# Split-precision matmuls in two passes per weight unit, high parts first and the low part last, with another order of loads and sums at the input stages' start

## The reference

```python
x = x + 0.5 * swiglu_ffn(x, ffn1_norm, ffn1_w_in, ffn1_w_out)   # D_FF = 5632
proj = rms_norm(x, mix_norm) @ w_in                             # q, k, v of 16 heads
# 8 heads: mixture of dilated windows; 8 heads: differential attention; RMS norm per head
x = x + mixed @ w_out
x = x + 0.5 * swiglu_ffn(x, ffn2_norm, ffn2_w_in, ffn2_w_out)

def swiglu_ffn(x, g, w_in, w_out):
    h = rms_norm(x, g)
    gate, up = jnp.split(h @ w_in, 2, axis=-1)
    return (jax.nn.silu(gate) * up) @ w_out
```

## Time and profile before

| | us |
|---|---|
| median of 3 runs | 1826.44 (1824.80 to 1827.83) |
| the profiled execution | 1826.57 |
| its span, first to last instruction | 1824.9 |
| PE busy in it | 1807.9 (99%) |
| DVE busy | 1519.9 (83%) |
| ACT busy | 1120.8 (61%) |

### The profile page before, as it was taken

One profiled execution on the slowest core, in us unless ns is written; L12 is line 12 of the kernel. 1 busy time (PEld: TensorE's weight loads), 2 busy tenths in 40 slices (PEclk: granted clock), 3 DMA queues, 4 the chain that ended last, 5 costly groups with the idle time before them and its releaser, 6 DMA issues.

```text
span 1824.9 us, 21558 instructions
## 1 busy us (share of the span) xinstructions
PE 1807.9 (99%) x8167; PEld 1475.5 (81%) x8167; DVE 1519.9 (83%) x1676; ACT 1120.8 (61%) x1437; POOL 78.9 (4%) x113
## 2 busy tenths in 40 slices
PE   9899999999999999999999999999999999999999
PEld 8688888888888888888888888788888888888887
DVE  6899999998889888667666666899999999889976
ACT  6666766666655555556556655566666666666453
POOL 0000000000000000111010000000000000000000
PEclk9999999999999999999999999999999999999999
DMA  9677776776545556654555445677777776554653
GB/s 361 183 245 221 238 246 218 228 226 202 182 171 206 209 207 209 207 180 149 171 165 183 152 161 193 229 237 246 243 224 241 241 228 189 186 184 162 237 201 139
DMA packets 184199, 378.62 MB, mean 207 GB/s; under 512 B 7824, under 2 KB 8864, under 8 KB 183840
## 3 DMA queue, kind: packets, MB, share of 16 engines
q1 hardware_dynamic: 178304, 351.02, 55.4%
q0 software_dynamic: 5760, 26.22, 7.5%
q10 hardware_dynamic: 32, 0.01, 0.0%
HBM read 348.91 MB, written 2.10 MB: 192 GB/s over the span
## 4 chain that ended last, share of the span: by engine, by line
PE 94%; DVE 3%; DMA 1%; issue 1%; SPq 1%; ACT 0%; POOL 0%; DVEq 0%; ACTq 0%; POOLq 0%
PE acc L587 13%; PE acc L588 13%; PE acc L589 13%; PE acc L649 6%; PE acc L650 6%; PE acc L651 6%; PE turn L665 5%; PE turn L667 5%; PE turn L668 5%; PE acc L665 4%; PE acc L667 4%; PE acc L668 4%; PE turn L618 1%; PE turn L787 1%; PE turn L786 1%; PE turn L788 1%
## 5 line engine op out<-in xcount | busy, mean ns | idle before, releaser
L1041 ACT ACTIVATE w_hi<-b 128x1024 fp32r<-128x1024 f32 (+1 forms) x300 | 268.8, 914 | 146.6 <-PE acc L651 113.4
L1436 DVE TENSOR_TENSOR w_lo<-b,w_hi 128x1024 fp32r<-128x1024 f32 (+1 forms) x300 | 298.1, 1043 | 53.5 <-ACT w_hi L1041 51.2
L1426 DVE TENSOR_TENSOR w_lo<-w_raw,w_hi 128x1024 fp32r<-128x1024 f32 x159 | 195.2, 1238 | 124.0 <-ACT w_hi L1017 123.5
L1017 ACT ACTIVATE w_hi<-w_raw 128x1024 fp32r<-128x1024 f32 x158 | 166.9, 1060 | 189.3 <-PE acc L589 166.7
L1055 ACT ACTIVATE w_hi<-w_raw 128x1024 fp32r<-128x1024 f32 x184 | 193.7, 1059 | 139.4 <-PE acc L589 96.4
L1446 DVE TENSOR_TENSOR w_lo<-w_raw,w_hi 128x1024 fp32r<-128x1024 f32 x184 | 223.1, 1222 | 43.0 <-ACT w_hi L1055 40.2
L587 PE MATMUL acc<-w_hi,h_hi 128*128 128x512 f32 x496 | 196.5, 396 | 0.2 <-DVE w_lo L1426 0.2
L589 PE MATMUL acc<-w_hi,h_lo 128*128 128x512 f32 x496 | 193.3, 390 | 0.0
L588 PE MATMUL acc<-w_lo,h_hi 128*128 128x512 f32 x496 | 193.2, 390 | 0.0
L649 PE MATMUL acc<-w_hi,h_hi 128*128 128x512 f32 x480 | 188.6, 393 | 0.3 <-DVE w_lo L1436 0.3
L588 PE MATMUL acc<-w_lo,act_hi 128*128 128x512 f32 x480 | 188.9, 393 | 0.0
(11 more groups left out here) (235 smaller groups left out, 3521.0 us busy)
## 6 DMA issues: line engine op xcount, KB each, us to landing
b<-in_ffn_w_in SPq DMA_DIRECT2D x80, 1280.0 KB, 5.8
w_raw<-in_ffn_w_out SPq DMA_DIRECT2D x88, 1024.0 KB, 5.5
w_raw<-in_ffn_w_in SPq DMA_DIRECT2D x54, 1024.0 KB, 5.3
w_raw<-in_w_in SPq DMA_DIRECT2D x48, 1024.0 KB, 5.1
w_raw<-in_ffn_w_in SPq DMA_DIRECT2D x44, 512.0 KB, 6.1
w_raw<-in_w_out SPq DMA_DIRECT2D x16, 1024.0 KB, 5.1
b<-t POOLq DMA_DIRECT2D x20, 768.0 KB, 7.8
b<-t POOLq DMA_DIRECT2D x20, 512.0 KB, 4.6
```

Of the source, the lines that this page charges most:

```text
L1017: nc.scalar.activation(w_hi[:, u % RING, 0:count, :], w_raw[:, slot, k0:k0 + count, :], ACT.Copy).then_inc(hi_ready, 1)
L1041: nc.scalar.activation(w_hi[:, u % RING, 0:count, :], in_raw(piece)[:, k0:k0 + count, :], ACT.Copy).then_inc(hi_ready, 1)
L1426: nc.vector.tensor_tensor(w_lo[:, slot, 0:count, :], w_raw[:, v // 2 % RAW, k0:k0 + count, :], w_hi[:, slot, 0:count, :].bitcast(F32), ALU ...
L1436: nc.vector.tensor_tensor(w_lo[:, u % RING, 0:count, :], in_raw(piece)[:, k0:k0 + count, :], w_hi[:, u % RING, 0:count, :].bitcast(F32), A ...
```

## The change

1. In `unit`, `plain_unit`, `form` and `out_form` a unit becomes two passes. PE waits for the high part only, issues hi x w_hi and lo x w_hi for all slices (and halves), then waits for the low part and issues hi x w_lo. The number of matmuls is the same. The first four units of IN1, written out apart, are not touched.
2. IN1's loads: chunk 6 moves ahead of B12 and chunk 7 ahead of B22 and B21.
3. IN2's loads: the four blocks move ahead of chunks 6 and 7.
4. On DVE the low parts of P1 come before `first_sum` (which `load_loop` then has to wait for by itself before B11 of the next loop), and `lambda_sums` comes after loop 0.
5. In a loop `make_u3` comes one low part earlier, before the last unit of P3.

```diff
                 if later:
+                    if i == 0:
+                        sp.wait_ge(sum_ready, (SUMS if s_in == IN2 else 0) + 1)
                     load_in(src, s_in, i + 1, B11, LAST[i, "P1"])
...
                 if s_in == IN2:
-                    load_first(gate_up, s_in)
-                    for piece in (B11, B12, B22, B21, G0, G1, U1, U0):
+                    load_first(gate_up, s_in, 0, RAW + 2)
+                    for piece in (B11, B12, B22, B21):
+                        load_in(gate_up, s_in, 0, piece)
+                    load_first(gate_up, s_in, RAW + 2)
+                    for piece in (G0, G1, U1, U0):
                         load_in(gate_up, s_in, 0, piece)
...
             load_first(gate_up1, IN1, RAW, RAW + 2)
-            for piece in (B11, B12):
+            load_in(gate_up1, IN1, 0, B11)
+            load_first(gate_up1, IN1, RAW + 2, RAW + 3)
+            load_in(gate_up1, IN1, 0, B12)
+            load_first(gate_up1, IN1, RAW + 3)
+            for piece in (B22, B21, G0):
                 load_in(gate_up1, IN1, 0, piece)
-            load_first(gate_up1, IN1, RAW + 2, RAW + 3)
-            for piece in (B22, B21):
-                load_in(gate_up1, IN1, 0, piece)
-            load_first(gate_up1, IN1, RAW + 3)
-            load_in(gate_up1, IN1, 0, G0)
...
             def unit(u, k0, count, lhs, bank, first, last, halves=False):
 
-                pe.wait_ge(lo_ready, u + 1)
                 slot = u % RING
+                pe.wait_ge(hi_ready, u + 1)
                 for kk in range(count):
                     for t in range(TT):
-                        hi, lo = (a[:, k0 + kk, t * P:(t + 1) * P] for a in lhs)
-                        o = banks[bank][:, t, :]
-                        nc.tensor.matmul(o, hi, w_hi[:, slot, kk, :], start=first[t] and kk == 0, stop=False)
-                        nc.tensor.matmul(o, hi, w_lo[:, slot, kk, :], start=False, stop=False)
-                        mm = nc.tensor.matmul(o, lo, w_hi[:, slot, kk, :], start=False,
-                                              stop=last[t] and kk == count - 1)
-                        if halves and kk == count - 1 and t == 0:
-                            mm.then_inc(first_half, 1)
+                        for n, a in enumerate(lhs):
+                            nc.tensor.matmul(banks[bank][:, t, :], a[:, k0 + kk, t * P:(t + 1) * P], w_hi[:, slot, kk, :],
+                                             start=first[t] and kk == 0 and n == 0, stop=False)
+                pe.wait_ge(lo_ready, u + 1)
+                for t in range(TT):
+                    for kk in range(count):
+                        mm = nc.tensor.matmul(banks[bank][:, t, :], lhs[0][:, k0 + kk, t * P:(t + 1) * P],
+                                              w_lo[:, slot, kk, :], start=False, stop=last[t] and kk == count - 1)
+                    if halves and t == 0:
+                        mm.then_inc(first_half, 1)
                 mm.then_inc(units_used, 1)
...
-                split_in_lo(s_in, LAST[i, "P6"] + 4, LAST[i, "P7"] + 4)
+                split_in_lo(s_in, LAST[i, "P6"] + 4, LAST[i, "P7"] + 3)
                 make_u3(s_in, n, i)
-                split_in_lo(s_in, LAST[i, "P7"] + 4, LAST[i, "GC"] + 1)
+                split_in_lo(s_in, LAST[i, "P7"] + 3, LAST[i, "GC"] + 1)
...
                     split_sums(n)
-                    lambda_sums()
                 else:
...
+                split_in_lo(s_in, 0, 3)
                 first_sum(s_in, n, 0)
-                split_in_lo(s_in, 0, 3)
...
                 for i in range(IN_LOOPS):
                     hidden(s_in, i, n)
+                    if n == 0 and i == 0:
+                        lambda_sums()
```

More of the change, by code:

```diff
@@ L658, in form @@
                     u = UNIT[s_in] + IN_FIRST + v
-                    pe.wait_ge(lo_ready, u + 1)
                     slot = u % RING
                     k0, count = IN_ORDER[v][3:]
+                    pe.wait_ge(hi_ready, u + 1)
                     for kk in range(count):
-                        hi, lo = lhs(k0 + kk)
-                        last = stop and k0 + kk == KS - 1
-                        nc.tensor.matmul(o, hi, w_hi[:, slot, kk, :], start=start and k0 + kk == 0, stop=False,
-                                         skip_group_check=True)
-                        nc.tensor.matmul(o, hi, w_lo[:, slot, kk, :], start=False, stop=False, skip_group_check=True)
-                        mm = nc.tensor.matmul(o, lo, w_hi[:, slot, kk, :], start=False, stop=last, skip_group_check=True)
+                        for n, a in enumerate(lhs(k0 + kk)):
+                            nc.tensor.matmul(o, a, w_hi[:, slot, kk, :], start=start and k0 + kk == 0 and n == 0,
+                                             stop=False, skip_group_check=True)
+                    pe.wait_ge(lo_ready, u + 1)
+                    for kk in range(count):
+                        mm = nc.tensor.matmul(o, lhs(k0 + kk)[0], w_lo[:, slot, kk, :], start=False,
+                                              stop=stop and k0 + kk == KS - 1, skip_group_check=True)
                     mm.then_inc(units_used, 1)
@@ L780, in out_form @@
             def out_form(u, lhs, o, start, stop):
+                slot = u % RING
+                pe.wait_ge(hi_ready, u + 1)
+                for kk in range(UK):
+                    for n, a in enumerate(lhs):
+                        nc.tensor.matmul(o, a[:, kk, :], w_hi[:, slot, kk, :], start=start and kk == 0 and n == 0, stop=False)
                 pe.wait_ge(lo_ready, u + 1)
-                slot = u % RING
                 for kk in range(UK):
-                    hi, lo = (a[:, kk, :] for a in lhs)
-                    nc.tensor.matmul(o, hi, w_hi[:, slot, kk, :], start=start and kk == 0, stop=False)
-                    nc.tensor.matmul(o, hi, w_lo[:, slot, kk, :], start=False, stop=False)
-                    mm = nc.tensor.matmul(o, lo, w_hi[:, slot, kk, :], start=False, stop=stop and kk == UK - 1)
+                    mm = nc.tensor.matmul(o, lhs[0][:, kk, :], w_lo[:, slot, kk, :], start=False, stop=stop and kk == UK - 1)
                 mm.then_inc(units_used, 1)
```

15 lines of the change are left out of this document (9 added, 6 removed).

## The result

| | before | after |
|---|---|---|
| median, us | 1825.62 (1824.73 to 1827.83, 4 runs) | 1810.64 (1810.57 to 1810.82, 4 runs) |
| span of the profiled execution | 1824.9 | 1809.1 |
| PE busy | 1807.9 | 1796.2 |

The ratio is 0.9916, with a 95% interval of 0.9899 to 0.9933: faster by 15.0 us. The forecast was 1809.1 in a range of 1800 to 1818. A negative number is a gain.

A forecast was written before the change was run, and what follows sets the result against it. TensorE, busy 99%, was taken as the bound, with only its holes to win. Terms -7.7 - 8.0 + 0.6 - 0.7 + 0.2 + 0.3 - 2 = -17.3 from 1826.57 gave 1809.3, by the median 1809.1 us; range 1800 to 1818.

The forecast's parts named there:

- Loops: Input-stage loops: PE's stalls for low parts at UA (18 x 0.23) and P7 (20 x 0.18) vanish, gaining 7.7 us.
- First start: Start of the first input stage: DVE's chain ends earlier, transposes after P2 at 67.9 instead of 75.95, gaining 8.0 us.
- Two parts are independent of each other: First input stage's start: moving `lambda_sums` and the earlier weight chunk each gain 3.8 us, independently.
- Added waits: About 920 new waits inside units, mostly on reached semaphores, cost 0.3 us for all.
- Rival (d): An added wait inside a unit costs as a stalled one does; all give 1809 + 74 = 1883 us; chance 0.03.
- Spacing: Steps between matmuls shrink because more followers stream from the same tile; -2 us taken, bounds -10 and +33.
- Rival (f): Matmul spacing doesn't depend on order within a unit but on where tiles lie; 1811.3 us, chance 0.20.
- (a): Only half the first input stage's start gain, as the chunk stays transfer-bound or DVE stalls elsewhere; 1813.3 us, chance 0.12.
- (b): Input loops don't get shorter: DVE at 92% sets them and the stall returns mid-unit; 1817.3 us, chance 0.12.
- (c): Slower: new pairs of load and stream cost more in the high pass; 1844 us, chance 0.05.
- (e): All matmuls take 389 ns, 10 us less; 1801 us, chance 0.05.
- (g): Gains and spacing cancel to within 0.2% (3.7 us); chance 0.03.

The follow-up runs named there:

- chunk_back: Changed kernel with the first input stage's loads in the order of before; 1813.45 us, ratio 0.9929.
- lambda_back: Changed kernel with `lambda_sums` put back behind `split_sums(n)`, ahead of the loops; 1817.34 us, ratio 0.9952.
- sum_early_2: Changed kernel with `first_sum` ahead of P1's low parts again in the second input stage only; 1809.22 us, ratio 0.9907.
- passes_only: Kernel before with only the units in two passes; loads, sums, `lambda_sums` and `make_u3` as before; 1816.31 us, ratio 0.9946.
- place_0: Changed kernel with gains and small vectors behind the large tiles, so act, mix, s_hi and raw weights begin at 0 modulo 1024; 1799.34 us, ratio 0.9852.
- best_order: Changed kernel with DVE's first sums earlier in both input stages and the first loop's third sum behind P2's low parts; 1811.81 us, ratio 0.992.
- best_all: best_order with tiles placed as in place_0 and the first loop's accumulating transfers waiting only for the sum they read; 1795.38 us, ratio 0.9836.

## Why the prediction was right, and where not

The total was 1809.1 for a measured 1810.64 (1.5 us off in 15.0, in the range). Against the profiled execution the sum was -17.3 and the trace shows -15.8. The close total owes something to luck: the loops gave 0.8 more than their term, the first start 0.8 less. Step by step:

- **Loops, -7.7.** Measured -8.5, of which 0.3 is the event at 228 us that the prediction did not count. The mechanism is shown by the runs: 41.37 with the passes alone, 41.80 with the order alone. The 0.23 and 0.18 per place (0.41 in a loop with both) came out as 0.43.
- **First start, -8.0.** Measured -7.2. The chain of 18.2 us measured 18.4 (49.97 to 68.40). It began 0.7 late. The sum had PE at unit 11 at 40.2, and it was there at 40.68, with no stall ahead of it. Of these 0.45 us, 0.11 is the restart, which the sum took off although it comes only after unit 11 has begun (the step into unit 11 was 0.63 in the trace of before, a stall of 0.40). The other 0.34 is there from the first microseconds on: one and the same matmul starts between 6.99 and 7.59 in the fourteen kernels here, and one and the same low part on DVE between 39.31 and 39.95; the term took one execution's start for exact. The last 0.2 is the time from the end of unit 11 on PE (43.40) to ScalarE's start on unit 15 (43.66), for which the sum had nothing.
- **"Two parts are independent of each other: 3.8 (lambda) and 3.8 (chunk)."** This step was wrong, though the sum was not. chunk_back and lambda_back show 2.6 for the chunk if `lambda_sums` is gone, and nothing if not. The row with the 3.07 us held the answer: a wait for a transfer ends at a time of its own, and what stands ahead of it can't be shortened with profit. The two had to be counted in that order: first the wait goes, then the chain behind it can move. Had the change left `lambda_sums` where it was, this step would have promised some 4.2 us at the first turn (8.0 - 3.8), where lambda_back has 0.7.
- **Second start, +0.6.** Measured +0.62; sum_early_2 shows the cause and takes it back.
- **The other wait, -0.7, and the end, +0.2.** Both as measured. A like wait at 654.77 in OUT1 (0.18 of the -0.26 there) was not in the sum.
- **Added waits, +0.3; make_u3, 0.** Measured 0.00: 138 of the 914 units with an added wait lie between 700 and 1130 us, and no turn moved against another there; at 0.08 each they would have cost 11 us. Rival (d) is out. `make_u3` was not undone by itself; the loops of passes_only (without it) and of the changed kernel are both 41.37, so it is worth nothing.
- **Spacing, -2.** Measured 0 in the output stages and between 700 and 1130 us; in the loops it can be no more than the 0.4 by which they gained more than the stalls. This is the mis-sized term: more than the whole 1.5 us of the miss. Rival (f), with 0.20, was right that the order within a unit doesn't matter, and its words on the cause, the differences "come from where the tiles lie", are borne out as far as place_0 goes. By the rule of the Trainium skill ("TensorE: Matmul & The Clock Gate", "Step-by-step: what each phase is for"), that loading the next weights takes no read bandwidth from the running matmul, this term was to be nothing, and the trace agrees (0.00 us from 700 to 1130 us with another order of loads and streams). The differences of 4 to 7 ns between the groups, which the prediction set against that rule, are averages over a pattern: on act the steps go 229.0, 231.2, 226.6 and again, in the old order and in the new. In the old one each kind of matmul fell on one place of that pattern, so the pattern showed up as a difference between lines (393, 392, 389); in the new one it spreads over them (392, 392, 391). The groups by line could not tell the two apart; the steps in order of time could. The high pass on act, at 392, is also where a sign of the prediction's list failed ("at or below 391"). And the term's two bounds don't belong together: +33 counts 7,440 matmuls from a middle of 391.5, from which all at 389 would be -19 and not -10.
- **Rivals (a) and (b)** did not come about, nor did (c), (e) and (g): the time is 9 us and more from the number of each of these three. In (a) it was the share of DMA that spoke for a chunk that stays late; the high parts of its units no longer waited for it. In (b) DVE's 92% is 93% now, and it costs nothing.

## What to carry to other kernels

A wait belongs where the data is first needed: a split of each unit into a pass on what is ready and a pass on what comes last hid some forty short stalls of 0.2 us, and its satisfied waits cost nothing that could be measured. Before two gains on one chain are added, ask which of them is a wait that ends at a time of its own; a gain ahead of it is worth nothing until it is gone. When steps differ by one or two per cent between tiles, look at where the tiles lie before explaining it by the order of instructions: here it was worth 11 us, three quarters of the whole change. And when work is moved back, look at who counts it: a queue that waits for "all sums" will follow, and can run into a load that has come forward.

## What the runs showed of the hardware that was not expected

- The step of matmuls with a weight load each depended on where tiles lie in a partition: 226.8 ns on act with act, mix, s_hi and the raw weights at 0 modulo 1024 bytes, 228.9 at 960, 232.7 to 233.4 at 896, 928 and 992. Moving these tiles by 32 bytes cost 9.8 us of 1810, moving them to a multiple of 1024 gave 11.3. Two loaded tiles that were never moved changed their step as well (233.3 and 226.7), so which tile's place does it is open.
- At 960 the step follows a pattern with a period of three matmuls (on act 229.0, 231.2, 226.6), whichever part is loaded or streamed; at 0 it is 226.9, 227.1, 226.2.
- A wait whose semaphore has been reached costs PE nothing measurable (0.00 us for 138 of them between 700 and 1130 us), while a wait that stalls costs its stall and a restart of 0.08 to 0.11.
- The granted clock fell after holes in PE's work of 2.25 us (chunk_back: 0.52 from 60 to 65 us), 2.36 us (best_order: 0.68 from 90 to 95 us) and 2.96 us (lambda_back: 0.73 from 60 to 70 us), with matmuls 0.43 us apart for some microseconds, and stayed at 1.00 with holes up to 1.3 us (the changed kernel).
- Two transfers that overlap: a load of 1.31 MB landed 5.5 us after its issue where the accumulating transfer had just ended (best_all), 8.1 us where it ran beside it for 3 us (the changed kernel) and 11.7 us where it did so for 8 us (best_order).
